# Sixty-four-wide head products on two quarters of TensorE, and state updates between inverse levels, in an RWKV scan

## What is computed

```python
def rwkv7_scan(r, w, k, v, a, b):
    def step(state, xs):
        r_t, w_t, k_t, v_t, a_t, b_t = xs
        sa = jnp.einsum('bhvk,bhk->bhv', state, a_t)
        state = state * w_t[:, :, None, :] + sa[..., None] * b_t[:, :, None, :] + v_t[..., None] * k_t[:, :, None, :]
        return state, jnp.einsum('bhvk,bhk->bhv', state, r_t)
    ...
wkv = rwkv7_scan(r, w_f, k, v, a_vec, b_vec) + flip_t(
    rwkv7_scan(flip_t(r), flip_t(w_b), flip_t(k), flip_t(v), flip_t(a_vec), flip_t(b_vec)))
```

## Time and profile before

| | |
|---|---|
| median of 3 runs | 7684.15 us (7682.7 to 7684.18) |
| span of the profiled execution | 7682.5 us |
| TensorE matmuls busy | 5907.2 us, 77% |
| TensorE weight loads busy | 4405.7 us, 57% |
| VectorE busy | 3557.0 us, 46% |
| ScalarE busy | 1231.8 us, 16% |
| GpSimd busy | 428.5 us, 6% |

### The profile page before, as it was taken

The page is one execution under the profiler, slowest core; times in us unless marked ns, Lnnn a source line. Parts: engine busy times, 40 slices in busy tenths (PEclk is TensorE's granted clock), DMA queues, the critical chain, the costliest instruction groups (busy, mean ns, idle before and its releaser), DMA issues. The chain is left out here.

```text
span 7682.5 us, 76452 instructions
## 1 busy us (share of the span) xinstructions
PE 5907.2 (77%) x27896; PEld 4405.7 (57%) x27896; DVE 3557.0 (46%) x4543; ACT 1231.8 (16%) x1880; POOL 428.5 (6%) x290
## 2 busy tenths in 40 slices
PE   6878851999963689677878867977657896869998
PEld 4768851999952467433333545854244454658877
DVE  7436657444455457474434343231534444542233
ACT  2102222222221110030000021001012233311100
POOL 0000002000000000022212000000200000000000
PEclk8989985999986899758989988988556678989999
DMA  1221123111213135233042212224311002232233
GB/s 72 82 78 33 33 83 144 35 42 33 44 54 132 34 134 186 75 115 140 33 148 77 101 39 82 98 77 141 103 25 26 21 5 54 85 106 69 73 111 124
DMA packets 370202, 604.35 MB, mean 79 GB/s; under 512 B 167180, under 2 KB 233739, under 8 KB 369084
## 3 DMA queue, kind: packets, MB, share of 16 engines
q1 hardware_dynamic: 279512, 412.30, 17.1%
q10 hardware_dynamic: 74592, 132.66, 4.7%
q0 software_dynamic: 15968, 57.78, 2.1%
HBM read 410.46 MB, written 192.19 MB: 78 GB/s over the span
## 5 line engine op out<-in xcount | busy, mean ns | idle before, releaser
L385 PE MATMUL gu_ps<-kept_h_hi,gu_w_hi 128*128 128x512 f32 x704 | 274.8, 390 | 39.6 <-DVE gu_w_lo L118 39.6
L1941 PE MATMUL lc_ps<-lc_tabi,lc_z 128*128 128x512 f32 x512 | 229.6, 612 | 69.3 <-issue 69.3
L385 PE MATMUL gu_ps<-kept_h_lo,gu_w_hi 128*128 128x512 f32 x704 | 274.6, 390 | 0.0
L385 PE MATMUL gu_ps<-kept_h_hi,gu_w_lo 128*128 128x512 f32 x704 | 274.5, 390 | 0.0
L385 PE MATMUL win_ps<-kept_hn_hi,win_w_hi 128*128 128x512 f32 x576 | 224.9, 391 | 39.6 <-DVE win_w_lo L118 39.6
L861 PE MATMUL rk_banka<-rk_xt,rk_ys 128*128 128x128 f32 x1280 | 230.1, 276 | 0.0
L852 PE MATMUL rk_bankc<-rk_x,rk_off 128*128 128x128 f32 x1280 | 176.5, 281 | 65.4 <-DVE rk_xt L840 41.8
L385 PE MATMUL win_ps<-kept_hn_lo,win_w_hi 128*128 128x512 f32 x576 | 224.8, 390 | 0.0
L385 PE MATMUL win_ps<-kept_hn_hi,win_w_lo 128*128 128x512 f32 x576 | 224.6, 390 | 0.0
L1927 PE MATMUL lc_ps<-lc_v,lc_tab 128*128 128x512 f32 x512 | 222.3, 592 | 0.0
L1941 PEld LDWEIGHTS lc_ps<-lc_tabi,lc_z 128*128 128x128 f32 x512 | 100.3, 197 | 198.5 <-issue 198.3
(11 more groups left out here) (637 smaller groups left out, 14403.1 us busy)
## 6 DMA issues: line engine op xcount, KB each, us to landing
oproj_mod_w<-in_ada_w POOLq DMA_DIRECT2D x12, 2048.0 KB, 9.5
gu_w<-in_w_gu SPq DMA_DIRECT2D x44, 512.0 KB, 3.5
rk_bd<-s_decayed SPq DMA_DIRECT2D x64, 320.0 KB, 4.3
win_w<-in_w_in SPq DMA_DIRECT2D x36, 512.0 KB, 3.6
s_z<-win_o ACTq DMA_DIRECT2D x36, 512.0 KB, 2.6
s_decayed<-rkp_ring SPq DMA_DIRECT2D x32, 512.0 KB, 2.7
dn_kv<-s_qkv SPq DMA_DIRECT2D x16, 768.0 KB, 6.3
wo_w<-in_w_out SPq DMA_DIRECT2D x24, 512.0 KB, 4.6
```

The costliest lines, as they stand in the source:

```text
L385: mm = pe.matmul(ps[:, u, h, :], a, b, start=(k == 0 and n == 0), stop=(k == kt - 1 and n == len(pairs) - 1))
L1941: mm = pe.matmul(ps[:, 0, 2 * (ct % 2) + e, :], z[:, kind, ft, ct * P:(ct + 1) * P], tabi[:, kind, ft, :], start=(n == 0), stop=(n == 7))
```

## The change

The head pairs are held compactly: a tile is 128x256, the first head of each pair on partitions 0 to 63 and the second on 64 to 127, with no zero blocks. A new helper, `by_head`, issues each product of a pair as two products of 64x64 with 64 columns, whose operands start at partition 0 and write to partition 0, or start at 64 and write to 64. All have one line, L1376. The transposes become such products with an identity.

The state work of chunk k is no longer behind the levels of chunk k, but stands in the instruction stream of chunk k + 1: the reading of the state beside Y of level 0, the solve before Z of level 1, and outputs and state's addition behind Y of level 2. What must live longer (`vb`, `kt`, `aa`, `xt`, `g`) has two buffers. The masked matrices of levels 1 to 5 are made by one GpSimd instruction per chunk and direction (L1416), 1280 elements wide; that of level 0 stays on VectorE. The inputs come for four chunks at a time (GROUP), in two buffers; y is gathered for four chunks and stored by SP. The loops over the chunks are written out in Python, so that no engine has a loop of its own there.

```diff
+        def by_head(pe, out, *terms):
+            for h in range(RPAIRS):
+                for n, (a, b) in enumerate(terms):
+                    for e in range(2):
+                        own = slice(RH * e, RH * e + RH)
+                        mm = pe.matmul(out[own, h, :], a[own, h, :], b[own, h, :], start=(n == 0), stop=(n == len(terms) - 1))
+            return mm
...
+                def load(q):
+                    for d in range(2):
+                        if q >= 2:
+                            sp.wait_ge(per[d]["y_out"], GROUP * (q - 1))
...
+                        sp.dma_start(to[:, 0:24, :], split(decayed[d])).then_inc(per[d][f"in{q % 2}"], 16)
+                        sp.dma_start(to[:, 24:28, :], split(shared[2:3])).then_inc(per[d][f"in{q % 2}"], 16)
...
             def _(pool):
-                for d in range(2):
-                    pool.memset(bd[d][:, :, :, :], 0.0).then_inc(zeroed, 1)
+                for i in range(RCH):
+                    for d in range(2):
+                        pool.wait_ge(per[d]["aa_ready"], i + 1)
+                        pool.wait_ge(per[d]["y_done"], i * LV)
+                        pool.tensor_tensor(off[d][:, 1:, :, :],
...
+                def begin(d, i):
...
+                    by_head(pe, Y[:, first, :], (piece(d, i, 1), piece(d, i, 0)))
+                    by_head(pe, Y[:, second, :], (piece(d, i, 2), piece(d, i, 0))).then_inc(s["aa"], 1)
+                    by_head(pe, A[:, first, :], (piece(d, i, 6), one))
+                    by_head(pe, A[:, second, :], (piece(d, i, 3), one)).then_inc(s["vb_turned"], 1)
+                    by_head(pe, DD[:, first, :], (piece(d, i, 4), one)).then_inc(s["k_turned"], 1)
...
+                def level_y(d, i, l):
...
+                    else:
+                        pe.wait_ge(s["off_rest"], i + 1)
+                        pe.wait_ge(s["x_ready"], i * XN + 2 * l)
+                    by_head(pe, Y[:, first, :], (off[d][:, l, :, :], b["x"][:, :, :] if l else one)).then_inc(s["y_done"], 1)
...
+                def level_z(d, i, l):
...
+                    pe.wait_ge(s["ys_copied"], i * (LV - 1) + l)
...
+                    if l < LV - 1:
+                        by_head(pe, DD[:, first, :], (t["xt"], b["ys"]))
+                    by_head(pe, A[:, first, :], (b["ys"], t["xt"])).then_inc(s["z_done"], 1)
...
+                def outputs(d, k):
...
+                    by_head(pe, G[:, first, :], (t["vb"][:, second, :], b["u"]), (t["kt"], t["vb"][:, first, :]))
+                    by_head(pe, G[:, second, :], (b["s"], piece(d, k, 5)), (b["u"], gk[:, first, :]),
+                            (t["vb"][:, first, :], gk[:, second, :])).then_inc(s["y_out"], 1)
+
+                for i in range(RCH + 1):
+                    inner, outer = i < RCH, i > 0
...
+                    for d in range(2):
+                        if inner:
+                            level_y(d, i, 0)
+                        if outer:
+                            read_state(d, i - 1)
+                    for d in range(2):
+                        if inner:
+                            level_y(d, i, 1)
+                    for d in range(2):
+                        if outer:
+                            solve(d, i - 1)
+                        if inner:
+                            level_z(d, i, 1)
+                    for d in range(2):
+                        if inner:
+                            level_y(d, i, 2)
+                        if outer:
+                            outputs(d, i - 1)
+                    if inner:
+                        for d in range(2):
+                            level_z(d, i, 2)
+                        for l in range(3, LV):
+                            for d in range(2):
+                                level_y(d, i, l)
+                            for d in range(2):
+                                level_z(d, i, l)
```

More of the change, by code:

```diff
@@ L1337, in rwkv @@
     LV = 6
+    XN = 2 * LV - 1
+    GROUP = 4
+    GT = GROUP * RH
     with Stage(nc, tag) as st:
[L1339 to L1345, removed]
@@ L1346, in rwkv @@
-        per = [{n: st.sem(f"{n}{d}") for n in names} for d in range(2)]
[L1347 to L1352, removed]
+        ident, masks = st.sb("ident", [P, RH]), st.sb("masks", [P, 2, LV, RH])
@@ new lines, in rwkv, with piece, chunk, pairs @@
+        off = [st.sb(f"off{d}", [P, LV, RPAIRS, RH]) for d in range(2)]
+        g = [[st.sb(f"g{d}{u}", [P, 2 * RPAIRS, RH]) for u in range(2)] for d in range(2)]
+        y = [[st.sb(f"y{d}{u}", [P, RPAIRS, GT]) for u in range(2)] for d in range(2)]
+        def piece(d, i, n):
+            j = i % GROUP if d == 0 else GROUP - 1 - i % GROUP
+            return given[d][i // GROUP % 2][:, n, :, j * RH:(j + 1) * RH]
+        def chunk(d, i):
+            return i if d == 0 else RCH - 1 - i
+        def pairs(t):
+            return t.unsqueeze(1).to_broadcast([P, RPAIRS, RH])
@@ new lines, in _ @@
+                load(0)
+                load(1)
+                for q in range(RCH // GROUP):
+                    for d in range(2):
+                        at = GT * (q if d == 0 else RCH // GROUP - 1 - q)
+                        sp.wait_ge(per[d]["y_copied"], GROUP * (q + 1))
+                        sp.dma_start(tiled(dst[d])[:, :, at:at + GT], y[d][q % 2][:, :, :]).then_inc(per[d][f"stored{q % 2}"], 16)
+                    if q + 2 < RCH // GROUP:
+                        load(q + 2)
@@ L1401, in _ @@
[L1401 to L1409 removed]
+                            s = per[d]
@@ L1415, in _ @@
                 dve.wait_ge(state_zeroed, 2)
-                dve.wait_ge(zeroed, 2)
                 dve.wait_ge(const_in, 64)
-                with dve.Fori(0, RCH) as i:
-                    chunk = [i, dve.snap(i * -1 + (RCH - 1))]
+                for i in range(RCH + 1):
+                    inner, outer, k = i < RCH, i > 0, i - 1
+                    for d in range(2):
+                        s, t = per[d], turns[d][i % 2]
+                        if inner:
+                            dve.wait_ge(s["aa"], i + 1)
+                            dve.wait_ge(s["off_rest"], i - 1 if i else 0)
+                            if i >= 2:
+                                dve.wait_ge(s["read"], i - 1)
+                            dve.tensor_tensor(t["aa"][:, :, :], banks[d][1][:, :, :],
+                                              strict[:, d, :].unsqueeze(1).to_broadcast([P, 2 * RPAIRS, RH]),
+                                              ALU.mult).then_inc(s["aa_ready"], 1)
+                            dve.wait_ge(s["aa_ready"], i + 1)
+                            dve.wait_ge(s["y_done"], i * LV)
+                            dve.tensor_tensor(off[d][:, 0, :, :], t["aa"][:, first, :], pairs(masks[:, d, 0, :]),
+                                              ALU.mult).then_inc(s["off_first"], 1)
```

280 lines of the change are left out of this document (144 added, 136 removed).

## The result

The changed kernel takes **7315.07 us** (median of 4 runs, 7310.33 to 7316.48) against 7684.16 for the kernel before (median of 4 runs, 7682.7 to 7691.28): a ratio of 0.951, 95% interval 0.9498 to 0.9522, 369 us less. The forecast was 7302. The profiled execution took 7314.5 us, with a span of 7313.0.

What follows compares the result with a forecast made beforehand. TensorE's stream was taken to bound the rwkv scan stage; first load 37, 16 chunks of 31, less 7, plus 12 and 2 gave 540 us against 921.9, so 7302 us; own range 7240 to 7360, 8 in 10 within 7240 to 7660.

Steps and rivals of the forecast that it cites:

- Step 1: TensorE's products in the rwkv scan: twice the passes at half the size, 28 ns each with two quarters side by side.
- Rival C: TensorE's quarters don't run side by side: 53 to 56 ns a pass, time 7642 to 7682 us; chance 0.15.
- Rival D: Sequencer's price per pass makes it slower, from 57 ns; at 107 to 111 ns, 8450 to 8511 us; chance 0.13.
- the alternation of the products: TensorE's stream: products alternate between two quarters sharing neither rows nor columns, a reason for 28 ns a pass.
- Step 2: One inverse level: its chain of waits shows, 3.4 us against 2.7 of stream for both directions.
- Step 3: State work moved into the next chunk's levels 0 to 2 fills waits: 31 us a chunk, 1 for handoffs.
- Step 4: VectorE 11.6 us and ScalarE 8.1 a chunk, hidden; GpSimd masks some 4.1 us each, perhaps 0.3 late.
- Step 5: Transfers: the first load takes 37 us (31 to 43), later loads are hidden, only the last store, some 3 us, is seen.
- Step 6: The scan's loop written out: waits compare with constants, no branch is left, costed at nothing.
- The sum: The stage: 37 + 16 x 31 - 7 + 12 + 2 = 540 us against 921.9, 382 us less.
- TensorE waiting for instructions: A sign of the forecast being wrong, if TensorE waited for instructions at each chunk.
- A granted clock below 1.00 in the steady part: A sign of the forecast being wrong, in the scan's steady part, where the clock was 1.00 before.

Runs made afterwards that it cites:

- quarters-in-turn kernel: The changed kernel with all products of the first quarter issued before those of the second, instead of alternating at each product: 7448.64 us, ratio 0.9696.
- groups of two: The changed kernel with GROUP = 2 in place of 4, so loads and stores are half as large and twice as many: 7316.74 us, ratio 0.9524.

## Why the prediction was right

The mechanism was right: the quarters overlap, TensorE's stream stays the bound, and the stage gives the whole gain. That the sum came within 13 us owes something to luck, since terms of 10 to 25 us were off in both directions.

- **Step 1, the price of a pass.** Taken as 28 ns; it is 29.2, two passes every 58.3 ns. That it goes with TensorE's clock shows at the stage's start: at a granted clock of 0.50 (1320.10 to 1321.90) 32 passes take 1.73 us (1320.13 to 1321.86), 54 ns each, nearly double. Rival C falls (its chunk of 52.3 us at 53 ns is 51.9 by its own sum; nothing rests on that): both quarters of a product write the same bank, and they run side by side. The Trainium skill, TensorEngine Tiling (Array Packing), Restrictions and Gotchas, says that different row tiles cannot access one PSUM bank at once; the trace disagrees for two tiles that share neither rows nor columns. Rival D falls as well. The Trainium skill, TensorE: Matmul & The Clock Gate, Part 2, gives some 62 ns per matmul where the sequencer decodes in software; 29.2 ns rules that out for this stream. The prediction gave the alternation of the products as one of its reasons; the quarters-in-turn kernel shows what it is worth.
- **Step 2, the level.** 3.4 us predicted, 3.48 measured. The additions of 256 start 0.34 us apart (1577.64, 1577.98; taken 0.33), and beyond its 2.80 us of stream TensorE is held up 0.68 us a level, where 0.7 was foreseen; 0.25 of it is the wait for VectorE that the profile shows in front of the second Y.
- **Step 3, the chunk.** 31 us with 1 us for handoffs; undisturbed it is 30.57. Two errors cancel here. The 960 passes take 28.0 us instead of 26.9, by the price of a pass; the waits between them take 2.5 us instead of 4.1, so the handoffs were counted too dear. Over 16 chunks that is 18 us one way and 25 the other. The move itself gives 23 us of the stage's 372.
- **Step 4, the other engines.** All hidden, as said. GpSimd's masks take 3.1 us instead of 4.1 (an x2 row of 6.18), and among TensorE's waits of the steady part none is for them.
- **Step 5, the loads: the term of the sum that was mis-sized.** The first load took 27.2 us to direction 1's first product instead of 37, at 299 and 348 GB/s where 171 and 234 were taken: 10 us less. "Later ones have over 100 us and are hidden" was wrong. The data are in time, but the loads hold up TensorE's instructions: 18.7 us by the kernel that leaves them out.
- **Step 6, the written-out loop, costed at nothing.** It is the other half of the same miss. The steady part had 3 instruction packets in 880 us and has 110 in 468 now. In the loop before, TensorE had no wait by "issue" of its matmuls in the list of that stretch's waits. The prediction took TensorE waiting for instructions as a sign of being wrong, if it came at each chunk; it came at the two beside the later loads. A granted clock below 1.00 in the steady part, another of its signs, came with them (1626 to 1628 us). That the writing-out is the cause was not tested by itself, with a loop around the new products; what is shown is that late instruction packets go with the stalls, and that the loads make them late.
- **The sum.** 540 us of stage were predicted, 550.2 measured. The first products of direction 1 in chunk 0 and of direction 0 in chunks 1 and 15 divide the stage:

```profile
1330.64 1.97 PE L1376 MATMUL rk_banky<-rk_in 64*64 64x64 f32 x32 [5.98 <-DMA rk_in<-s_rk_shared]
...
1358.94 1.15 PE L1376 MATMUL rk_banky<-rk_in 64*64 64x64 f32 x32
...
1809.86 1.15 PE L1376 MATMUL rk_banky<-rk_in 64*64 64x64 f32 x32
```

The first load took 27.2 us (predicted 37), the rest of chunk 0 28.3 (31 - 7 = 24), chunks 1 to 14 450.9, a mean of 32.2 (14 x 31 = 434), and chunk 15 with the end 43.7 (31 + 12 + 2 = 45). So the start gave 10 us back, and chunks 0 to 14 took 21 more than they were given, of which the later loads are some 19 by the kernel without them. Chunk 0 ran its first products at a granted clock of 0.50 and stood 2.1 us by "issue" beside the load of group 1 (at 1346). The other 3 us of the 13 are outside the stage, where the runs themselves differ by more.

## What to carry to other kernels

When a kernel of many small products leaves the issue of instructions no slack, look at the instruction queue beside the data queues: a large load that is early enough for its data can still stall the engine by what stands ahead of its instructions. Cut it into pieces of some 1.5 us, paced by the engine that it would disturb. Two diagonal quarters of the array double the rate of 64x64 products in f32, but only if they alternate in the instruction stream. Here they alternate at every product; runs of 8 passes on each quarter gave up a quarter of the rate (36 ns a pass against 29.2).

## What the runs showed of the hardware

- Two 64x64 quarters on the diagonal overlap almost completely, also into one PSUM bank: 29.2 ns a pass against 58 for one quarter alone and 112 for a 128x128 product. A quarter of the array takes half the time of the whole.
- TensorE was seen to start passes on a free quarter only about three passes ahead of their turn: with blocks of 8 on each quarter 16 passes cost 0.58 us instead of 0.47.
- Instruction packets keep their length beside a load (1.07 us) but come every 6.7 us instead of 3.75, and TensorE stands up to 2.8 us at a time, 4.2 in the kernel with groups of two.
- Behind one such stall of 2.81 us the granted clock fell to 0.50 for some 3.3 us, and 64 passes took 3.29 us instead of 1.87. Behind others of 2.67 and 2.70 us it stayed at 1.00.
- Loads of 7.34 MB in four calls cost TensorE some 9 us each (17.5 us by "issue" for two); in fourteen paced pieces some 2 (6.2 us for three).
- VectorE's operation of 256 columns on the level-0 mask (L1588) took 1.13 us when it started while GpSimd's masks ran (1690.87), and 0.42 when it started ahead of them (1688.54). It was not on the path here.
